# The last chunk's keys projected ahead of its queries, and short and long chunks alternated in latent attention

## What is computed

```python
proj = h @ w_in
c_q = rms_norm(proj[..., :384], cq_norm)
c_kv = rms_norm(proj[..., 384:640], ckv_norm)
k_rope = proj[..., 640:]
q = (c_q @ w_uq).reshape(bsz, seq, 8, 192)
kv = (c_kv @ w_ukv).reshape(bsz, seq, 8, 256)
k_nope, v = kv[..., :128], kv[..., 128:]
k = concatenate([k_nope, broadcast(k_rope)], axis=-1)
q, k = rms_norm(q, q_norm), rms_norm(k, k_norm)      # then rotary on the last 64
s = q @ k.T * scale                                  # causal mask
o = softmax(s) @ v
x = x + o @ w_o
x = x + hierarchical_moe(rms_norm(x, ffn_norm), ...) # top 2 of 64 experts a token
```

## Time and profile before

| | us |
|---|---|
| median of 3 runs | 1480.46 (1474.95 to 1480.96) |
| the profiled execution | 1482.28 |
| its span in the trace | 1480.5 |
| first score of the attention | at 842.35 |
| first output product | at 914.59 |
| end of the output projection | at 969.79 |

### The profile page before, as it was taken

The page is one execution under the profiler, slowest core; times in us unless marked ns, Lnnn a source line. Parts: engine busy times, 40 slices in busy tenths (PEclk is TensorE's granted clock), DMA queues, the critical chain, the costliest instruction groups (busy, mean ns, idle before and its releaser), DMA issues.

```text
span 1480.5 us, 16899 instructions
## 1 busy us (share of the span) xinstructions
PE 1248.6 (84%) x6452; PEld 579.9 (39%) x6452; DVE 621.5 (42%) x1208; ACT 258.1 (17%) x520; POOL 79.8 (5%) x81
## 2 busy tenths in 40 slices
PE   6989999997776875977999899998996877876777
PEld 5556455333232332322564566463332222322232
DVE  7998135534232232333306573154532223232233
ACT  5245111000000000000335653120000000000000
POOL 2013001000000000000000000001000000000000
PEclk9999999999898898998999899999998988988899
DMA  6101937799999999999510306257999999999996
GB/s 226 57 1 31 387 131 298 304 420 420 420 420 420 420 420 420 421 405 394 208 57 0 128 1 257 112 199 302 394 419 420 420 421 421 419 421 420 416 396 238
DMA packets 78019, 447.32 MB, mean 302 GB/s; under 512 B 10607, under 2 KB 12799, under 8 KB 29424
## 3 DMA queue, kind: packets, MB, share of 16 engines
q1 hardware_dynamic: 69536, 428.54, 71.2%
q0 software_dynamic: 6384, 11.32, 2.1%
q10 hardware_dynamic: 2016, 6.34, 1.1%
HBM read 450.54 MB, written 6.29 MB: 309 GB/s over the span
## 4 chain that ended last, share of the span: by engine, by line
PE 49%; DMA 36%; DVE 8%; SPq 4%; issue 2%; ACT 1%; DVEq 0%; POOLq 0%; ACTq 0%
DMA ring<-in_moe_w 22%; PE ps L1609 18%; DMA region_a<-in_moe_w 12%; PE ps L497 4%; SPq L1798 4%; PE ps L1646 3%; PE ps L944 3%; PE ps L964 2%; PE ps L1635 2%; PE ps L370 2%; PE ps L968 2%; PE ps L446 2%; PE ps L486 2%; DMA con<-in_p_const 1%; PE ps L1018 1%
## 5 line engine op out<-in xcount | busy, mean ns | idle before, releaser
L1609 PE MATMUL ps<-ring,region_b 128*32 128x512 f32 (+1 forms) x1216 | 305.2, 659 | 99.9 <-DMA ring<-in_moe_w 58.5
L1646 PE MATMUL ps<-region_b 128*128 128x512 f32 x576 | 256.8, 599 | 1.4 <-ACT region_b L1706 1.4
L1724 DVE TENSOR_TENSOR x<-ps,x 128x512 f32<-128x512 f32 x288 | 199.2, 692 | 53.3 <-PE ps L1646 49.8
L1735 DVE TENSOR_TENSOR scr<-scr,ps 128x256 f32<-128x256 f32 x38 | 16.0, 421 | 471.1 <-ACT scr L1699 471.1
L1609 PE MATMUL ps<-wbuf,region_b 128*32 128x512 f32 x288 | 150.3, 682 | 65.5 <-DMA ring<-in_moe_w 65.5
L1609 PEld LDWEIGHTS ps<-ring,region_b 128*32 128x32 f32 (+1 forms) x1216 | 81.4, 129 | 254.1 <-issue 251.3
L1646 PEld LDWEIGHTS ps<-region_b 128*128 128x128 f32 x576 | 106.5, 190 | 152.0 <-issue 148.8
L1609 PE MATMUL ps<-extra,region_b 128*32 128x512 f32 x288 | 150.4, 683 | 0.0
L1635 PE MATMUL ps<-ring,scr 128*32 128x512 f32 (+1 forms) x704 | 132.7, 601 | 15.0 <-DVE scr L1741 15.0
L1609 PE MATMUL ps<-region_a,region_b 128*32 128x512 f32 x256 | 136.3, 694 | 0.0
L1699 ACT ACTIVATE scr<-ps 128x256 f32<-128x256 f32 x38 | 14.6, 384 | 460.5 <-PE ps L1609 460.5
(11 more groups left out here) (325 smaller groups left out, 1593.2 us busy)
## 6 DMA issues: line engine op xcount, KB each, us to landing
ring<-in_moe_w SPq DMA_DIRECT2D x232, 1024.0 KB, 21.2
wbuf<-in_moe_w SPq DMA_DIRECT2D x76, 1024.0 KB, 19.3
extra<-in_moe_w SPq DMA_DIRECT2D x36, 1024.0 KB, 21.1
region_a<-in_moe_w SPq DMA_DIRECT2D x32, 1024.0 KB, 23.5
ring<-in_moe_w SPq DMA_DIRECT2D x16, 512.0 KB, 10.2
wbuf<-in_ev_w_in SPq DMA_DIRECT2D x3, 2048.0 KB, 15.6
wbuf<-in_ev_w_out SPq DMA_DIRECT2D x2, 2048.0 KB, 14.9
hrow<-region_a ACTq DMA_DIRECT2D x8, 512.0 KB, 10.5
```

The costliest lines, as they stand in the source:

```text
L1609: last = TE.matmul(ps[r, 2, :], xtr[:, k, r], up_weights(UP_SLOT[t], k), start=k == 0, stop=k == KC - 1)
L1646: TE.matmul(ps[:, SUMS[i % 4], :], back[:, i // 2, :], yo[:, (i % 2) * 512:(i % 2 + 1) * 512], start=True, stop=True).then_inc(s_cb, 1)
L1724: V.tensor_tensor(xs, ps[:, SUMS[i % 4], :], xs, ALU.add).then_inc(s_ca, 1)
```

## The change

The projection's order is changed for the last chunk: its key-value units come ahead of chunk 2's transposes, its query units behind them; its transposes begin with the keys (3, 4, 5), then the queries (0, 1, 2). The rotary keys' squares are taken once, for all chunks, ahead of the projection. The scaling of the keys is one instruction in each half. The last chunk's query factors are computed after the fourth head of the attention. The scores of pairs 0 and 1 (chunk 0) are issued ahead of the last transposes.

The attention's pairs go in the order `PAIRS`, in which chunk 0 and chunk 3 alternate, then 1 and 3, then 1 and 2. ScalarE copies head n-4's transposed weights before head n's exponential. Results are copied out pair by pair. The first two output products (chunk 0) are issued between the last pairs, and the eight products use eight banks.

```diff
-        SBANK = (0, 1, 2, 7)
+        SBANK = (0, 1, 2, 3)
+        PAIRS = [(0, 0), (0, 1), (0, 2), (3, 0), (0, 3), (3, 1), (1, 0), (3, 2), (1, 1), (3, 3), (1, 2), (2, 0),
+                 (1, 3), (2, 1), (2, 2), (2, 3)]
+        HEADS = [(c, 2 * p + j) for c, p in PAIRS for j in range(2)]
...
-        for c in range(TC + 1):
-            if c < TC:
-                UNITS += [("q", c, n) for n in range(3)] + [("kv", c, n) for n in range(4)]
+        for c in range(TC - 1):
+            UNITS += [("q", c, n) for n in range(3)] + [("kv", c, n) for n in range(4)]
             if c:
                 UNITS += [("t", c - 1, n) for n in range(6)]
+        UNITS += [("kv", TC - 1, n) for n in range(4)] + [("t", TC - 2, n) for n in range(6)]
+        UNITS += [("q", TC - 1, n) for n in range(3)] + [("t", TC - 1, n) for n in (3, 4, 5, 0, 1, 2)]
...
-            for u in range(len(UNITS) - 8, len(UNITS)):
-                TE.wait_ge(*copied(u))
...
+                if u == len(UNITS) - 2:
+                    odd_scores(0)
+                    odd_scores(1)
+            for g in range(2, H * TC // 2 + 3):
+                if g < H * TC // 2:
+                    odd_scores(g)
                 for m in (2 * g - 4, 2 * g - 3):
...
+                if g >= H * TC // 2:
+                    n = g - H * TC // 2
+                    if n < 2:
+                        TE.wait_ge(s_ex, H * TC - 3 + n)
+                        TE.wait_ge(s_oe, OUT_AT[0])
+                        out_product(n)
+            TE.wait_ge(s_oe, H * TC // 2)
+            TE.wait_ge(s_ex, H * TC)
+            for n in range(2, 8):
+                out_product(n)
...
+            if g == 2:
+                for u in range(len(UNITS) - 4, len(UNITS)):
+                    TE.wait_ge(*copied(u))
...
+            S.wait_ge(s_cn, TC)
+            for c in range(TC):
+                S.activation(sq[:, 1024 + c * ROPE:1024 + (c + 1) * ROPE], kro[:, c, :], ACT.Square,
+                             accum_out=krss[:, c:c + 1])\
+                    .then_inc(s_krs, 1)
...
             for n in range(H * TC + 4):
+                m = n - 4
+                if m >= 0:
+                    nk = (HEADS[m][0] + 1) * P
+                    S.wait_ge(s_pt, m + 1)
+                    if m >= 4:
+                        S.wait_ge(s_o, m - 3)
+                    S.activation(pT[m % 4][:, 0:nk], ps[:, 4 + m % 2, 0:nk], ACT.Copy).then_inc(s_pte, 1)
                 if n < H * TC:
...
-                m = n - 4
-                if m >= 0:
...
+            c = TC - 1
+            key_copies(c)
+            key_sums(c)
+            V.wait_ge(s_hr, TC)
+            vlink(V.reciprocal(hrs[:, 8:16], hroot[:, 8:16]))
+            key_scale(c)
+            V.wait_ge(*copied(unit("q", c, 2)))
+            rotation(c, 0)
+            rotation(c, 1)
+            query_sums(c)
+
+            def last_scale():
+                V.wait_ge(s_hr, TC + 1)
+                vlink(V.reciprocal(hrs[:, 0:8], hroot[:, 0:8]))
+                score_scale(TC - 1)
...
+                    if n == 4:
+                        last_scale()
...
-                if n >= 10 and n % 4 == 2:
-                    g = (n - 10) // 4
-                    V.wait_ge(s_o, 4 * g + 4)
...
+                if n >= 8 and n % 2 == 0:
+                    g = (n - 8) // 2
+                    V.wait_ge(s_o, 2 * g + 2)
...
-            sp.wait_ge(s_q, unit("kv", TC - 1, 3) + 1)
+            sp.wait_ge(s_q, unit("q", TC - 1, 2) + 1)
...
-            sp.wait_ge(s_op, 9)
+            sp.wait_ge(s_op, 11)
             up_load(1, 5)
...
-                    g.wait_ge(s_kn, TC)
+                    g.wait_ge(s_kn, 2 * TC)
+                    g.wait_ge(s_qn, TC)
                     row_gain(3)
```

More of the change, by code:

```diff
@@ L488, in even_tensor @@
                 last.then_inc(s_op, 1)
[L490 to L499, removed]
         def outproj_vector(layer):
@@ L1006, in odd_tensor @@
                             TE.wait_ge(s_pte, m - 1)
-                        for b in range(m // H + 1):
-                            last = TE.transpose(ps[:, 3 + m % 2, b * P:(b + 1) * P],
+                        for b in range(HEADS[m][0] + 1):
+                            last = TE.transpose(ps[:, 4 + m % 2, b * P:(b + 1) * P],
                                                 pr[m % 6][:, b * P:(b + 1) * P], ident)
@@ L1021, in odd_tensor, with odd_scores, out_product @@
                         last.then_inc(s_o, 1)
-            TE.wait_ge(s_oe, 2 * TC)
-            outproj_tensor(lambda k, c: oT[:, k, c * P:(c + 1) * P])
+                if g >= H * TC // 2:
[8 more added lines that the diff above has]
+                out_product(n)
+        def odd_scores(g):
+            if g == 2:
+                for u in range(len(UNITS) - 4, len(UNITS)):
+                    TE.wait_ge(*copied(u))
+            if g < 2:
+                for u in (len(UNITS) - 8 + 2 * g, len(UNITS) - 7 + 2 * g):
+                    TE.wait_ge(*copied(u))
+            c = PAIRS[g][0]
+            nk = (c + 1) * P
+            cc = slice(c * P, (c + 1) * P)
+            for n in (2 * g, 2 * g + 1):
+                if n >= 4:
+                    TE.wait_ge(s_ex, n - 3)
+                TE.matmul(ps[:, SBANK[n % 4], 0:nk], qTn[:, HEADS[n][1], cc], kTn[:, HEADS[n][1], 0:nk],
+                          start=True, stop=False)
+            for n in (2 * g, 2 * g + 1):
+                r = slice(64 * (n % 2), 64 * (n % 2) + 64)
+                TE.matmul(ps[:, SBANK[n % 4], 0:nk], qTr[r, HEADS[n][1] // 2, cc], kTr[r, HEADS[n][1] // 2, 0:nk],
+                          start=False, stop=True).then_inc(s_sc, 1)
+        OUT_AT = [max(i for i, (c_, p_) in enumerate(PAIRS) if c_ == 0) + 1]
+        def out_product(n):
+            if n < 2:
+                TE.wait_ge(s_wb[n], 32)
+            for k in range(KC):
+                last = TE.matmul(ps[:, n, :], oT[:, k, (n // 2) * P:(n // 2 + 1) * P], wout[n % 2][:, k, :],
+                                 start=k == 0, stop=k == KC - 1)
+            last.then_inc(s_op, 1)
         def odd_ctrans(c):
```

150 lines of the change are left out of this document (79 added, 71 removed).

## The result

| | before | changed |
|---|---|---|
| median of 6 runs, us | 1476.85 | 1465.59 (1463.47 to 1469.50) |
| ratio to before, 95% interval | | 0.9917 (0.9899 to 0.9934) |
| span of the profiled execution, us | 1480.5 | 1464.9 |
| first query unit of the projection, us | 766.64 | 763.61 |
| from there to the first score | 75.71 | 68.97 |

The change makes the kernel 0.8% faster, 11 to 12 us; the forecast was 9.4. Three more runs of the kernel before lowered its median by 3.6 us, to 1476.85, so the forecast time of 1471.1 rested on a base that was too high, and the measured one lies at the fast edge of the range.

A forecast was written before the change was run, and what follows sets the result against it. TensorE was taken as the attention's bound. 899.5 + 3.6 low clock + 1.5 waits + 0.6 drain + 55.2 products = 960.4 against 969.8, 9.4 us earlier, giving 1471.1 us; range 1465 to 1479.

The forecast's parts named there:

- the order of the pairs: Attention: with alternating pairs VectorE stays a little under TensorE in nearly each step; without waits TensorE's work ends at 899.5.
- the one on the copies: ScalarE in the attention: copying ahead of exponentials takes one VectorE head (1.2 to 1.8 us) out of the loop; 1.5 us waits remain.
- step 3: TensorE's attention step g = 3 (scores g, transposes g-2, values g-3), from which TensorE was to be the bound.
- the 9.9 us lost ahead of the last score: Attention of the kernel before: 47.8 us of TensorE work took 57.7, blamed on VectorE's chunk 0 pace and low clock.
- the low clock: TensorE's clock at the attention's start: falls after idle time, full again from 852, 3.6 us lost (bounds 1.6 to 6.1).
- What bounds, and whether the gain arrives: Output projection to expert stage: the next load hangs on the eighth product, so the span gains what the projection's end gains.
- The third rival: Expert stage: its start hangs on the first experts' load at the last score, only 3 us gained, 1478; chance 0.05.
- Start: Attention's start: the reordered last units bring the first exponential at 841.2 in place of 845.29, a lead of 4.1 us.
- the rival built on that rule: ScalarE's table load: a drain of 1.3 to 1.4 us delays the first exponential, lead 2.7, 1472.5; chance 0.03.
- The rival in which the clock stays low to 871: Chunk 3's scores run at low clock until the 9.4 us margin is gone; slower, 1495 if low to 900; chance 0.05.
- The one in which it doesn't fall: Attention's start: TensorE's clock doesn't fall, nothing lost in place of 3.6, 13 us gained, 1467.5; chance 0.15.
- Drain: Attention's end, 4.6 us lost before: two products of 6.9 us cover the last heads, no clock fall, 0.6 us left.

The follow-up runs named there:

- e1: Changed kernel with the pairs of heads in the order of before; output projection ends 191.0 us after the first query unit (changed 190.6), ratio to before 0.9907.
- e5: Kernel before with only ScalarE's copy moved ahead of the exponential; output projection ends 195.1 us after the first query unit (before 203.0), ratio 0.9968.
- e2: Changed kernel with ScalarE's exponential again ahead of the copy; output projection ends 199.5 us after the first query unit (changed 190.6), ratio to before 0.9975.
- e6: Changed kernel plus three unused matmuls in TensorE's idle time ahead of the third pair; first query unit to projection's end 189.3 us (changed 190.6), ratio 0.9896.
- e8: Changed kernel plus four extra ScalarE copies ahead of the table load; first query unit to projection's end 192.9 us (changed 190.6), ratio to before 0.9917.
- e4: Changed kernel with the last chunk's old unit order and no late query scaling; first query unit to projection's end 193.4 us (changed 190.6), ratio 0.9933.
- products after: Also written e3: changed kernel with all eight output products behind the attention; first query unit to projection's end 190.0 us (changed 190.6), ratio 0.9900.
- e7: Also written before, clock kept: kernel before plus four unused matmuls in TensorE's hole ahead of the attention; first query unit to projection's end 200.6 us, ratio 0.9997.
- e12: Kernel before without VectorE's mask add in each head; first query unit to projection's end 197.1 us (before 203.0), one run of 1468.70 us.
- e13: Kernel before with ScalarE's copy ahead of the exponential and no mask add; first query unit to projection's end 193.9 us, one run of 1474.83 us.
- e9: Changed kernel with the pairs in the order of before and the exponential ahead of the copy; first query unit to projection's end 197.3 us, ratio 0.9948.
- e10: Changed kernel plus three unused matmuls ahead of the third pair, all eight products behind the attention; first query unit to projection's end 189.6 us, ratio 0.9886.
- e11: Same as e10 but with the pairs in the order of before; first query unit to projection's end 191.9 us, ratio to before 0.9897.

## Why the prediction was right or wrong

The step that failed is the one on the order of the pairs, with the one on the copies beside it. The prediction took alternation as the reason why TensorE would be the bound from step 3 on, and so as what wins back the 9.9 us lost ahead of the last score. The runs show 0.4 us for alternation (e1). In its place they show ScalarE's copy ahead of its exponential, which the prediction priced by one wait of 1.74 us: 7.9 us by itself in the kernel before (e5), 8.9 when undone in the changed one (e2). The term of the sum that was mis-sized most is the low clock, put at 3.6 us and measured at 1.3 (e6). By parts:

**What bounds, and whether the gain arrives.** Right. The load behind the eighth product moved with the projection's end, 15.4 us in both, and the part behind is the same to 0.2 us. The third rival, a gain lost in the expert stage, is out. The last score was put near 897 and ended at 894.1 on the clock of the trace before.

**Start.** Nearly right. The first exponential was put at 841.2 and came at 837.64, which is 840.7 on the clock of the trace before; a lead of 4.6 us for 4.1. Its chain is the forecast one: copy, square 1.49, six copies, table load, exponential. That the lead goes through was shown (e8, 2.24 of 2.53), and the part of it that is the units' order is 2.4 (e4). The scores of the first long pair were put at 844.8 and came at 843.9 in the same frame; I had them wait for the fourth head's exponential, but the first of their two matmuls needs the third's alone.

**Table load.** The rows above have the copy at 835.73 for 0.60, the load at 836.35 for 1.28, the exponential at 837.64. By the Trainium skill (ScalarE: Activation LUTs, What ACT_TABLE_LOAD costs) some 1.4 us of drain go with a switch; here there is 0.02 ahead of it and 0.01 behind. The trace disagrees, and the rival built on that rule (a lead of 2.7) is out.

**Low clock.** The mechanism was right, the size was not. It fell, as forecast, but was back at 844 (847 in the frame of before) and not at 852; the price is 1.3 us (e6) for 3.6. This is the term that was mis-sized most, 2.3 of the 3.0 us by which the stretch beat the forecast. The start makes 0.9 more, at the first long scores. TensorE's work and waits together came out as forecast, to 0.3 us on the long side (113.5 us from the first long scores to the end, less 55.2 of products, 1.3 of clock and 0.5 of the drain's rest, is 56.5 for 54.7 + 1.5). That the clock came back after 6.8 us is luck in part: `products after` had the same idle time and got it back after 3.4, the kernels with the start of before after 13.7 and 17.1. The rival in which the clock stays low to 871 was far off. The one in which it doesn't fall is out too, since it fell.

**Order of the pairs.** The sum used it as the reason why TensorE would be the bound from step 3 on. TensorE is the bound: it has no wait over 0.6 us from there. But e1 shows that it is so with the pairs in order too, 0.4 us later. I had read the 9.9 us lost before the last score as VectorE's pace in chunk 0 (1.18 us a head) and the low clock. VectorE's pace alone can't be it: in e1 the short heads stand first and cost 0.4 us. Nor is the low clock much of it: e7 took away 10 of the 17 us and won 0.8 there. The copy's place won 4.1 there (e5). The rest isn't split by a run.

**Copies ahead of exponentials.** This step failed by what it left out. It named the right chain (the transpose waits for a copy that waits for an exponential that waits for VectorE), and then gave it no number but the drain's 1.74. The view of waits had the rest: 4.3 us of TensorE for the copy at five places, and 6.9 of its weight loads for VectorE's result, while VectorE waited 14.5 us for scores. e5 measures 7.9 us for this part alone (4.7 in time), e2 8.9, and e12 with e13 support the chain. The total came near only because TensorE's work was summed forward, and that sum holds whichever part removes the waits. A forecast of the alternation alone by the same steps would have been wrong in sign with the old order of the copy (e9 against e2).

**Drain.** Put down as covered by two products. They hide 0.3 us (e3, and e10 beside e6). It was the copy's place that took the wait of 1.74 out (e5 has none in its drain, without products in it). Some 1.6 of the 4.6 us that I had counted as lost there were the fall of the clock, which e7 doesn't have behind the same wait, so that part of the gain may be owed to the one execution of before and not to the change. The forecast number for its rest, 0.6, is 0.52.

**Sum.** On the stretch 12.4 us for 9.4, or some 10.8 without the clock's fall in the drain of before. By parts, from the traces: the copy's place 6.3 to 8.9 (4.7 in time in the kernel before), the order of the last units 2.8, the rest of the start about 2, alternation 0.4, products in the drain 0.3. Each is the price of one part with the others in place, or alone, so they overlap and come to more than 12.4.

What stays open: why the clock came back after 7 us here, after 3.4 in e3 behind the same instructions, and after 17 before; what alternation is worth without a low clock, which e11 was to show and doesn't; and how the 0.8 us of e7 ahead of the last pair's scores are shared between the clock and the first exponential, which came 1.1 us earlier there.

## What to carry to other kernels

Where an engine has two streams in one queue, one that the bound engine waits for and one that waits for somebody slower, the first goes ahead; here that was worth more than any other part of the change. A wait that comes back at each step is to be priced over all its places, not by its longest one: the longest here was 1.74 us, the view of waits had 4.3 in the kernel before, and with the order undone in the changed kernel 9.0 for a loss of 8.9. And read the effect of an edit between two fixed instructions of the trace: here 2 us could be seen there that four runs of the whole could not tell (e8). But look at the granted clock of both traces first, as its low stretches moved the same instructions by 0.9 us and a drain by 1.6.

## What the runs showed of the hardware that was not expected

The granted clock of TensorE fell around or soon after a short idle time and stayed low for very different lengths: 2.6 us idle and 6.8 low in the changed kernel, the same 2.6 idle and 3.4 low in `products after`, whose instructions up to there are the same; 1.7 idle and 3.4 low in the drain of before, the same 1.7 idle and no fall in the drain of `before, clock kept`; and 17.1 low around the hole ahead of the attention of before, with TensorE busy 14.8 of these 17.

Three matmuls of 128x512 in the hole kept it at 1.00 in the changed kernel. The same three with the pairs in order didn't: it fell 78 us behind the first query unit for 6.8 us. Four in the kernel before put the fall off by 10 us and shortened it from 17.1 to 6.8.
